# Writing the end of one pair of heads into the next pair's rotation, in two attention mixers

## The reference, cut to what matters

```
def diff_mixer(q, k, v, lam_params, norm_g, lam_init, cos, sin):   # 4 heads, two maps each
    q = apply_rope(q...); k = apply_rope(k...)
    s = einsum('bqhmd,bkhmd->bhmqk', q_blk, k) * scale;  p = softmax(s)
    a = p[:, :, 0] - lam * p[:, :, 1]
    o = einsum('bhqk,bkhe->bqhe', a, v)
    return rmsnorm(o, norm_g) * (1.0 - lam_init)

def swa_mixer(q, k, v, sink, cos, sin):                            # 8 query heads, 2 key heads, window of 128
    q = apply_rope(q...); k = apply_rope(k...)
    p = exp(s - m) / (sum(exp(s - m)) + exp(sink - m))
    return einsum('bncgqk,bnkcd->bnqcgd', p, vw)
```

## Time and profile before

| what | value |
|---|---|
| median of three runs | 4163.24 us |
| the profiled execution | 4159.45 us |
| its span, first to last instruction | 4157.7 us |
| PE busy | 3544.2 us, 85% |
| DVE busy | 2308.1 us, 56% |
| ACT busy | 1375.3 us, 33% |
| POOL busy | 579.7 us, 14% |
| granted TensorE clock over the span | 0.918 of full |

### The profile page before, as it was taken

One profiled execution on the slowest core, in us unless ns is written; L12 is line 12 of the kernel. 1 busy time (PEld: TensorE's weight loads), 2 busy tenths in 40 slices (PEclk: granted clock), 3 DMA queues, 4 the chain that ended last, 5 costly groups with the idle time before them and its releaser, 6 DMA issues. The chain is left out here.

```text
span 4157.7 us, 48483 instructions
## 1 busy us (share of the span) xinstructions
PE 3544.2 (85%) x17648; PEld 2902.6 (70%) x17648; DVE 2308.1 (56%) x4342; ACT 1375.3 (33%) x2570; POOL 579.7 (14%) x450
## 2 busy tenths in 40 slices
PE   7787788778689999778878999889998779788997
PEld 6666666666568888557756888668887557576886
DVE  3555634656338875567663333347875667653333
ACT  3313333133323333333433232233332334424321
POOL 1000010000103332111111110103332100102100
PEclk9988899888899999889989999999999889899999
DMA  4531035311243221212333333342222212323332
GB/s 126 149 107 34 18 103 143 112 34 31 61 140 105 77 73 55 70 57 79 82 89 91 91 96 86 107 138 76 82 63 83 59 51 62 106 84 88 95 96 66
DMA packets 553874, 350.06 MB, mean 84 GB/s; under 512 B 73220, under 2 KB 497156, under 8 KB 553372
## 3 DMA queue, kind: packets, MB, share of 16 engines
q1 hardware_dynamic: 553628, 346.84, 29.3%
HBM read 301.36 MB, written 45.42 MB: 83 GB/s over the span
## 5 line engine op out<-in xcount | busy, mean ns | idle before, releaser
L658 PE MATMUL bank<-h,w_hi 128*128 128x512 f32 (+1 forms) x1728 | 761.2, 441 | 187.0 <-DVE w_low L651 158.4
L659 PE MATMUL bank<-h,w_hi 128*128 128x512 f32 (+1 forms) x1728 | 707.1, 409 | 0.0
L660 PE MATMUL bank<-h,w_low 128*128 128x512 f32 (+1 forms) x1728 | 707.1, 409 | 0.0
L658 PEld LDWEIGHTS bank<-h,w_hi 128*128 128x128 f32 (+1 forms) x1728 | 344.4, 199 | 285.0 <-DVE w_low L651 170.0
L645 ACT CAST w_hi<-w 128x1024 fp32r<-128x1024 f32 (+1 forms) x328 | 298.9, 913 | 456.9 <-DMA w<-in_w_in 295.4
L651 DVE TENSOR_TENSOR w_low<-w,w_hi 128x1024 fp32r<-128x1024 f32 (+1 forms) x328 | 372.2, 1136 | 77.8 <-ACT w_hi L645 72.8
L660 PEld LDWEIGHTS bank<-h,w_low 128*128 128x128 f32 (+1 forms) x1728 | 341.6, 198 | 82.3
L659 PEld LDWEIGHTS bank<-h,w_hi 128*128 128x128 f32 (+1 forms) x1728 | 345.1, 200 | 72.3 <-issue 9.6
L459 DVE TENSOR_TENSOR w_low<-w,w_hi 128x1024 fp32r<-128x1024 f32 x128 | 174.6, 1364 | 155.4 <-ACT w_hi L453 155.4
L1300 ACT ACTIVATE prob<-bank,softmax_stat 128x512 f32<-128x512 f32 (+3 forms) x256 | 145.2, 568 | 289.8 <-DVE softmax_stat L1332 224.8
L659 PE MATMUL bank<-yT_low,w_hi 128*128 128x512 f32 x512 | 215.6, 421 | 0.0
(11 more groups left out here) (435 smaller groups left out, 7152.8 us busy)
## 6 DMA issues: line engine op xcount, KB each, us to landing
w<-in_w_in SPq DMA_DIRECT2D x148, 512.0 KB, 4.2
w<-in_w_mlp SPq DMA_DIRECT2D x128, 512.0 KB, 4.0
z<-z_tile SPq DMA_DIRECT2D x164, 256.0 KB, 4.1
w<-in_w_gate SPq DMA_DIRECT2D x64, 512.0 KB, 4.1
q_twice<-z SPq DMA_DIRECT2D x128, 128.0 KB, 3.2
w<-in_w_branch SPq DMA_DIRECT2D x64, 256.0 KB, 2.9
k_twice<-z SPq DMA_DIRECT2D x88, 128.0 KB, 3.7
w<-in_w_out SPq DMA_DIRECT2D x32, 256.0 KB, 2.8
```

The source lines that it names most:

```text
L658: self.t.matmul(bank[0:n, :], wh, high, start=j == 0, stop=False)
L659: self.t.matmul(bank[0:n, :], wh, low, start=False, stop=False)
L660: return self.t.matmul(bank[0:n, :], wl, high, start=False, stop=j == self.depth(i) - 1)
```

## The change

In both mixers the first pair's tail becomes a generator of its own (`tail_pe`, `tail_act`, `tail_dve`), and a helper writes it between the pieces of the second pair's rotation. PE no longer waits for the tail's copies ahead of the rotation, but for the last exponential and the last copies of probabilities (the rotation writes the same PSUM banks); the wait for the tail's copies now stands ahead of the transposes of v. The yields around the first pair's tail go away on all engines, and the share rises from 0.85 to 0.9 in Diff and from 0.72 to 0.76 in Swa. The second pair's tail stays at the mixer's end. In Diff both of the last 2.0 yields stand around it, in Swa both of 1.0. SP writes the second pair's row DMAs right after the last attention step. `rows_dve` moves out of `heads_dve`, and Mlstm calls it itself, which leaves Mlstm as it was.

```diff
+def while_turning(rotation, tail):
+
+    for share in rotation:
+        next(tail, None)
+        yield share
+    for _ in tail:
+        pass
...
 class Diff(Attention, Rotation, NormedHeads):
-    score_banks, other_banks, share = 2, ((2, 3), (4, 5)), 0.85
+    score_banks, other_banks, share = 2, ((2, 3), (4, 5)), 0.9
...
     def pe(self):
...
             if p:
+                self.t.wait_ge(*self.expd(self.last(p - 1), 1))
+                self.t.wait_ge(*self.copied(self.last(p - 1)))
+            yield from while_turning(self.rotate_pe(p), self.tail_pe(p - 1) if p else iter(()))
+            if p:
                 self.t.wait_ge(*self.y_stored(p - 1, 1))
-            yield from self.rotate_pe(p)
...
-            yield 2.0
-            self.t.wait_ge(*self.h_normed(p))
-            self.rows_pe(p, self.y[:, :, :].rearrange("p (t j) d -> p t (j d)", j=2))
-            yield 2.0
+        yield 2.0
+        for _ in self.tail_pe(1):
+            pass
+        yield 2.0
+
+    def tail_pe(self, p):
+        for _ in range(4):
+            yield
+        self.t.wait_ge(*self.h_normed(p))
+        self.rows_pe(p, self.y[:, :, :].rearrange("p (t j) d -> p t (j d)", j=2))
+        yield
...
+    def tail_act(self, p):
+        self.a.wait_ge(*self.out_done(self.last(p)))
+        rows = self.k.yT[:, self.first + 2 * p:self.first + 2 * p + 2, :]
+        self.heads_act(p, self.y, rows.rearrange("p j (t n) -> p (j t) n", n=P))
+        yield
...
+    def tail_dve(self, p):
+        for _ in range(3):
+            yield
+        self.heads_dve(p, self.y, lambda i: self.gain[:, :])
+        yield
+        yield
+        self.rows_dve(p)
+        yield
...
 class Swa(Attention, Rotation, NormedHeads):
-    score_banks, other_banks, share = 2, ((2, 3), (4, 5)), 0.72
+    score_banks, other_banks, share = 2, ((2, 3), (4, 5)), 0.76
...
+    def tail_pe(self, p):
+        self.t.wait_ge(*self.out_done(self.last(p)))
+        self.rows_pe(p, self.y)
+        yield
...
+    def tail_dve(self, p):
+        yield
+        self.rows_dve(p)
+        yield
```

More of the change, by code:

```diff
@@ L3065, in heads_dve @@
         m.then_inc(self.h_normed.sem, 1)
-        self.rows_dve(p)
     def rows_pe(self, p, y):
@@ L3152, in sp @@
                 yield
-            yield
-            yield
+        yield
+        yield
     def pe(self):
@@ L3181, in act @@
         for p in range(2):
-            yield from self.rotate_act(p)
+            yield from while_turning(self.rotate_act(p), self.tail_act(p - 1) if p else iter(()))
             for j in range(2):
@@ L3187, in act @@
             yield from self.attend_act(p)
[L3188 to L3192, removed]
+        for _ in self.tail_act(1):
+            pass
+        yield
[5 more added lines that the diff above has]
+        yield
     def lambda_dve(self):
@@ L3217, in dve @@
         for p in range(2):
-            yield from self.rotate_dve(p)
+            yield from while_turning(self.rotate_dve(p), self.tail_dve(p - 1) if p else iter(()))
             yield
             yield from self.attend_dve(p)
-            yield
-            self.heads_dve(p, self.y, lambda i: self.gain[:, :])
-            yield
+        yield
+        for _ in self.tail_dve(1):
+            pass
+        yield
+    def tail_dve(self, p):
+        for _ in range(3):
+            yield
+        self.heads_dve(p, self.y, lambda i: self.gain[:, :])
+        yield
+        yield
+        self.rows_dve(p)
+        yield
     def pool(self):
@@ L3303, in pe @@
             if p:
+                self.t.wait_ge(*self.expd(self.last(p - 1), 0))
+                self.t.wait_ge(*self.copied(self.last(p - 1)))
+            yield from while_turning(self.rotate_pe(p), self.tail_pe(p - 1) if p else iter(()))
+            if p:
                 self.t.wait_ge(*self.y_stored(p - 1, 1))
-            yield from self.rotate_pe(p)
             self.t.wait_ge(*self.v_in(p))
@@ L3310, in pe @@
             yield from self.attend_pe(p)
[L3311 to L3314, removed]
+        yield 1.0
+        for _ in self.tail_pe(1):
+            pass
+        yield 1.0
+    def tail_pe(self, p):
+        self.t.wait_ge(*self.out_done(self.last(p)))
+        self.rows_pe(p, self.y)
+        yield
     def values_ready(self, eng, p):
```

## The result

The changed kernel is slower: 4183.76 us median (4171.04 to 4193.09, 12 runs) beside 4168.44 for the kernel before (4154.7 to 4181.93, 12 runs), ratio 1.0034, interval 1.0019 to 1.0049, so some 14 us. The forecast was 4153.2, 10 us less. The profiled execution took 4185.48 for a span of 4183.7, granted clock 0.913 for 0.918.

The account below looks back on a forecast made before the run. PE, busy 85% of the span, was taken as the bound, so gains come only from its idle or slow-clocked time. Both Diff layers -15.4 and both Swa layers +5.4 gave -10.0: 4163.2 to 4153.2 us, range 4143 to 4165.

Parts of the forecast that it names:

- Diff, first attention: Diff's first attention: one more halt stands in it and costs itself, +1.4 us, bounds -0.6 to +1.4.
- Diff, tail and second rotation: Diff, from the last values to the second pair's first scores: 32.2 us for 42.1, so -9.9 us.
- V: Zero point of the times: start of the first pair's last values on PE, before the change 1761.13 in Diff, 1934.07 in Swa.
- minus 1.6 for the stream's pieces: Term in DVE's 27.3 us for Diff's second rotation: later halts 35 and 36 and their pieces move out, -1.6 us.
- The lower bound: Diff's tail and second rotation at its smallest gain: DVE's 24.3+3.6 without relief and 3 us of waits, V+34.9 (-7).
- Diff, the end: Diff's end: shorter second tail wait, but one halt behind the transposes holds up the barrier; 0 to +1.6, middle +0.8 us.
- Swa (+2.7: Each Swa layer: extra halt +1.4, earlier rotation -2.0, rotation start to scores +3.3; in all +2.7 us, bounds 0 to +5.
- Rival 3: Slower: the tail breaks the rotation's ring of PE and DVE; +14 us in all, 4177; chance 10%.
- decision point: Rival 3 decides when PE comes to the transposes more than 7 us ahead of DVE; the prediction found 4.2.
- the ring: The second rotation as a loop of PE and DVE waiting for each other; one break priced at 3.90 us of DVE idle.
- Rival 1: POOL's products block the tail's scalings on DVE in Diff's rotation: +2.6 us for each Diff, 4158.4; chance 20%.
- Rival 2: Swa loses nothing, as its transposes lie in time DVE had to spare; -15.4 us alone, 4147.8; chance 12%.

## Why the prediction was wrong

**Diff, first attention (+1.4; measured +5.7 and +4.9).** The step failed. The price of the halt held where the clock stayed at 1.00 (1.4 us, second layer). What failed is the rest: I let every other step keep its time, and even allowed a better fed PE to win 2 us. With the shares alone, the tail unmoved, the attention is longer by 4.3 and 5.0 us. In the first layer that is 2.0 less 0.7 around the step that had no halt, 1.6 in a step that runs at 7.6 us for 6.0, and 1.4 in the last steps, which hold only transposes and values and where a halt has moved; in the second most of it lies in steps with the same work at a lower clock. The bounds "-0.6 to +1.4" were too narrow from above. The second attention, costed at nothing because its halts keep their number, gave +2.3 and +3.6. Kernels with its halts in the same places took 50.9 to 57.3 us there, and the unchanged class took 54.6 once for 52.2, so what sets it stays open.

**Diff, tail and second rotation (-9.9; measured -4.4 and -4.5).** The start held: first rotation matmul at V+2.6 for V+2.3, no wait for its row, ACT hidden, the gate unit's fetch hidden. Scalings ended at V+17.4 for V+15.5, and PE waited 4.88 for 4.2. The sum for VectorE failed: 27.3 from start to last low part, measured 31.2. The term "minus 1.6 for the stream's pieces" has the wrong sign, they are 0.9 more, so 2.5 us; idle time on PE's matmuls grew by 2.3 (3.8 for 1.55) where 1.0 stood. These two are 3.8 of the 3.9. The other 1.3 us stand behind the last low part: 2.8 us to the scores where one halt of 1.5 was forecast, because the gate unit that opened there waited 3.02 us and its halts ran at the lower clock. The lower bound was also added up wrong: with the halt behind the low part it is V+35.8 and not V+34.9, and the measured V+37.7 lies outside either.

**Diff, the end (+0.8).** +0.9 and +1.3: held.

**Swa (+2.7; measured +5.6 and +6.5).** The halt ahead of the first scores (+1.4, measured +2.0 and +1.5) and the earlier rotation (-2.0, measured -1.8 and -2.0) held, the wait of 4.3 us for the row was 4.41. Rotation to scores was forecast at +3.3 and came at +6.5 and +5.9. The step that failed is its sum for VectorE. Its second product moved by 4.9 and 3.8 us where +3.0 stood: behind the wait for the row the first rotation matmul, the transposes and the halt ran at the lower clock (2.05 us for 1.10, 1.92 for 1.04), which I had priced in the bound alone. From there to the low part that halt 31 waits for it took 2.4 us more where 1.3 for the copies less 0.4 for contention stood: that low part now stands behind the last one of the rotation and not ahead of it, and another, of 512 columns, took 1.75 us beside GpSimd for 0.68, so contention that I had subtracted came back in another instruction. Halt 31 is not the missing part, for the same halt waited 4.73 us in the kernel before; moved behind the scores, its time came back in the attention.

**The rivals.** Rival 3 had the sign, and a part of its mechanism: with share 0.85 the rotation is 5.8 us shorter once PE does not wait in its middle. That its +14 meets the difference of the medians is luck: it has +2.1 for a Diff that lost 4.3 and 4.7 and +5 for a Swa that lost 5.6 and 6.5. Its decision point did not hold, nor does its place: in the kernel after, moving the wait gives 1.6 us, and the tail put outside the ring costs as much. Rival 1 did not occur in the changed kernel, where the scalings took 2.19 us as before, because PE's own wait kept GpSimd still. It occurred as soon as that wait was moved: 5.12 against 2.19, and 2.19 again with GpSimd's product cut to 8 columns. The Trainium skill, "SBUF — State Buffer", section "SBUF: two separate sides", says that a VectorE operation with two inputs in SBUF, as these scalings are, and a GpSimd operation that reads SBUF hold each other up; these numbers agree. Rival 2, that Swa loses nothing, is true at 0.72 and not at 0.76.

**What stays open.** How much of Swa's later second product is the clock and how much the order of the queue was read from the trace and not tried by itself; nor was the row DMA moved ahead of the fetch with the share kept at 0.76. And why the same Swa takes 132 us behind one Diff and 136 behind another: its attentions take 39.6 or 41.2 us at a granted clock of 1.00 or 0.96, and no run separates what sets that phase. The same holds for Diff's second attention.

## What to carry to other kernels

Moving work into stalls also moves what lies between the stalls: find out which instruction the next halt is, not only how many there are. A halt that opens a unit waits for that unit's weights (6.91 us ahead of Diff's scores with the shares alone), and moving it only moves the wait if the engine that makes them stays as late. A row DMA written one halt later may stand behind a fetch: it came at V+6.4 and not at V+2.9. Change the place and the share one at a time; here Swa's tail alone made it faster, and with one more halt ahead of it the same tail made it slower. A queue that waits in order holds up everything written behind it, so a tail put "outside the ring" is paid with the halts behind it.

## What the runs showed of the hardware

A wait can protect its neighbour: eight scalings on VectorE took 2.19 us while GpSimd was kept still by PE's wait, and 5.12 us once it was not. A later step of Diff's attention with the same work takes 6.0 us at a granted clock of 1.00 and 7.6 at 0.78, and a piece of work that is too small to change the sum of PE's work (one halt in twelve steps) shifts which steps are the long ones: the attention with it took 4 to 5 us more, where the halt itself cost 1.4 at a clock of 1.00.
